# Three tiles instead of two ahead, and two gathered tiles instead of three beside the dense experts

## The reference

```python
v1, i1 = lax.top_k(s1, PEER_TOPK)
v2, i2 = lax.top_k(s2, PEER_TOPK)
cand = (v1[..., :, None] + v2[..., None, :]).reshape(nb, PEER_HEADS, PEER_TOPK * PEER_TOPK)
sc, sel = lax.top_k(cand, PEER_TOPK)
idx = jnp.take_along_axis(cidx, sel, axis=-1)
g = jax.nn.softmax(sc, axis=-1)
h = jnp.einsum('nd,nhkd->nhk', xb, u[idx]).astype(jnp.float32)
a = (jax.nn.gelu(h) * g).astype(xb.dtype)
return jnp.einsum('nhk,nhkd->nd', a, v[idx])
```

## Time and profile before

| | us |
|---|---|
| median of 3 runs | 4242.48 (4242.30 to 4243.69) |
| the profiled execution | 4242.34 |
| its span, first to last instruction | 4240.4 |
| early phases | 1 to 556 |
| late phases (projection, differential, window, merge, memory) | 556 to 1999 |
| late retrieval | 2000 to 2583 |
| experts | 2610 to 4209 |
| TensorE, VectorE, ScalarE, POOL busy | 3276.6, 3193.4, 1079.0, 1665.2 |

### The profile page before, as it was taken

The page is one execution under the profiler, slowest core; times in us unless marked ns, Lnnn a source line. Parts: engine busy times, 40 slices in busy tenths (PEclk is TensorE's granted clock), DMA queues, the critical chain, the costliest instruction groups (busy, mean ns, idle before and its releaser), DMA issues. The chain is left out here.

```text
span 4240.4 us, 46588 instructions
## 1 busy us (share of the span) xinstructions
PE 3276.6 (77%) x14797; PEld 2487.0 (59%) x14797; DVE 3193.4 (75%) x5977; ACT 1079.0 (25%) x1952; POOL 1665.2 (39%) x1349
## 2 busy tenths in 40 slices
PE   7677459986869788577645534999999999999995
PEld 6444448864547544365645534777777777777774
DVE  4311568665756487683689995999999999999997
ACT  3211121112313211111115443222222222222222
POOL 0000015653433255462000002666666666666663
PEclk9678779996975699797768878999999999999997
DMA  5222149987756787883001116999999999999996
GB/s 198 70 102 104 50 149 330 351 298 216 239 166 211 254 315 283 325 280 132 3 13 84 84 79 234 367 360 364 361 366 360 364 362 362 364 363 362 363 362 226
DMA packets 410032, 1047.07 MB, mean 247 GB/s; under 512 B 45472, under 2 KB 160800, under 8 KB 408864
## 3 DMA queue, kind: packets, MB, share of 16 engines
q0 software_dynamic: 184384, 672.09, 43.6%
q1 hardware_dynamic: 206080, 364.00, 23.9%
q10 hardware_dynamic: 19440, 9.44, 0.8%
HBM read 973.58 MB, written 72.88 MB: 247 GB/s over the span
## 5 line engine op out<-in xcount | busy, mean ns | idle before, releaser
L2059 POOL DMA_INDIRECT exp_gu<-in_peer_u_rows,exp_gidx x384 | 553.6, 1442 | 1055.8 <-DMA exp_ggate<-s_ggate 609.9
L2067 POOL DMA_INDIRECT exp_gv<-in_peer_v,exp_gidx x384 | 453.6, 1181 | 122.9 <-issue 116.8
L65 POOL DMA_INDIRECT H<-in_peer_u_rows,gidx x256 | 340.9, 1332 | 409.5 <-DVE dots L74 291.8
L2133 DVE SCALAR_TENSOR_TENSOR H<-exp_gv,exp_coef,H 128x1024 f32<-128x1024 f32 x384 | 470.7, 1281 | 14.3 <-issue 8.4
L2199 PE MATMUL exp_h<-exp_xh,exp_uh 128*128 128x512 f32 x1024 | 410.4, 401 | 89.2 <-ACT exp_gel L2088 48.9
L2123 DVE CUSTOM_DVE_ANT_0 exp_gu<-exp_gu,exp_xg 128x1024 f32<-128x1024 f32 x384 | 459.2, 1221 | 0.0
L2201 PE MATMUL exp_h<-exp_xh,exp_ul 128*128 128x512 f32 x1024 | 401.0, 392 | 0.0
L2200 PE MATMUL exp_h<-exp_xl,exp_uh 128*128 128x512 f32 x1024 | 400.0, 391 | 0.0
L74 DVE CUSTOM_DVE_ANT_0 H<-H,xg 128x1024 f32<-128x1024 f32 x256 | 301.8, 1221 | 33.1 <-DMA H<-in_peer_u_rows,gidx 32.9
L2207 PE MATMUL exp_y<-exp_vh,exp_ah 128*128 128x512 f32 x768 | 300.3, 391 | 0.0
L2208 PE MATMUL exp_y<-exp_vl,exp_ah 128*128 128x512 f32 x768 | 300.0, 391 | 0.0
(11 more groups left out here) (318 smaller groups left out, 6986.9 us busy)
## 6 DMA issues: line engine op xcount, KB each, us to landing
exp_u<-in_peer_u SPq DMA_DIRECT2D x128, 512.0 KB, 6.5
exp_v<-in_peer_v SPq DMA_DIRECT2D x128, 512.0 KB, 7.3
proj_w<-in_w_in SPq DMA_DIRECT2D x32, 1024.0 KB, 8.8
exp_w<-s_w SPq DMA_DIRECT2D x128, 256.0 KB, 6.4
out_z<-proj_zs SPq DMA_DIRECT2D x72, 256.0 KB, 5.8
merge_gates<-out_z SPq DMA_DIRECT2D x9, 1024.0 KB, 5.4
merge_wo<-in_w_out SPq DMA_DIRECT2D x2, 4096.0 KB, 29.3
top_wq<-in_w_peer_q SPq DMA_DIRECT2D x2, 4096.0 KB, 13.3
```

Source lines behind the costliest of these rows:

```text
L65: pool.indirect_dma_start(out=ring[j % len(ring)], out_offset=None, in_=table, in_offset=bass.IndirectOffsetOnAxis(ap=K["gidx"][:, u % NE, ...
L2059: pool.indirect_dma_start(out=gu[i % 2][t][:, :], out_offset=None, in_=I["peer_u_rows"], in_offset=bass.IndirectOffsetOnAxis(ap=gidx[:, t, ...
L2067: pool.indirect_dma_start(out=gv[i % 2][t][:, :], out_offset=None, in_=I["peer_v"].rearrange("a b d -> (a b) d"), in_offset=bass.IndirectO ...
L2133: dve.scalar_tensor_tensor(out=H[:, FIRST_G + t, :], in0=gv[x][t][:, :], scalar=coef[:, t:t + 1], in1=H[:, FIRST_G + t, :], op0=ALU.mult, ...
```

## The change

NE goes from 2 to 3 and NG from 3 to 2, so three tiles pass ahead, six follow, and of these two are gathered and four stay dense. The six lists of numbers are made for it: 384 dots are spread as 189, 111 and 84, and 384 axpys as 39, 189 and 156. The memory phase keeps five buffers (2 and NE). In the step of the experts the second addition now follows the last dot.

```diff
@@ -24,7 +24,7 @@
 CW = 512
 ROPED, PLAIN = 3, 5
 CHUNKS = ROPED + PLAIN + 1
-NE = 2
+NE = 3
 NKEY = 128
 
 
@@ -90,10 +90,10 @@
     return ap[:, bass.ds(c % 2, 1), 4 * half:4 * half + 4, 0:width].rearrange("p a k n -> p (a k) n")
 
 
-HIGH_AT = {2: (0, 0), 7: (3, 5)}
-LOW_AT = {2: (0, 0), 7: (4, 6)}
-LOAD_AT = {2: (1, 1), 7: (5, 7)}
-PER_TILE = (0.0, 2.0, 2.0, 2.6, 2.6, 2.6, 2.6, 2.6, 2.3)
+HIGH_AT = {3: (0, 1), 6: (2, 4)}
+LOW_AT = {3: (0, 1), 6: (3, 5)}
+LOAD_AT = {3: (1, 2), 6: (4, 6)}
+PER_TILE = (0.0, 3.0, 3.0, 4.3, 4.3, 4.3, 4.3, 4.3, 4.0)
 
 
 def phase_project(nc, sem, K, I, S, base, n, units=()):
@@ -1539,7 +1539,7 @@
                 output(n - 1)
 
 
-NG = 3
+NG = 2
 ND = NT - NE - NG
 PH = 8
 TOP = 16
@@ -2158,10 +2158,9 @@
                         add_half(q - 1, 1)
                     if further:
                         low_u(q + 2, s)
-                    dot(s, turn, 0)
-                    dot(s, turn, 1)
+                    for t in range(NG):
+                        dot(s, turn, t)
                     add_half(q, 0)
-                    dot(s, turn, 2)
                     if not first:
                         axpy(q - 1, 1 - s, turn_before)
 
@@ -2294,9 +2293,9 @@
                                base=0, pattern=[[-1, P]], channel_multiplier=1)
 
 
-DOTS = (140, 84, 32)
-AXPYS = (24, 124, 108)
-MERGE_SLOTS, MEMORY_SLOTS = 7, 3
+DOTS = (189, 111, 84)
+AXPYS = (39, 189, 156)
+MERGE_SLOTS, MEMORY_SLOTS = 7, 2
 
 
 def spans(counts):
```

## The result

The changed kernel takes 4376.82 us (median of 4 runs, 4376.38 to 4381.16), the kernel before 4243.08 on the same chip: a ratio of 1.0313, 95% interval 1.0299 to 1.0327. The profiled span went from 4240.4 to 4374.4 us, +134.0.

A forecast was written before the change was run, and what follows sets the result against it. It took VectorE to bound the experts' step, TensorE close behind, and gathers' 360 to 365 GB/s to limit the changed late phases. Early +180, late retrieval -45, late +134, experts -150: +119 on 4242.34, 4360 us; range 4260 to 4440.

The forecast's parts named there:

- the late term: Five late phases, projection to memory: losing a tile and gaining gathers, counted as bytes at the ceiling, costs +134 us.
- Experts, -150: Experts: step falls from 12.30 to 11.1 us, TensorE next at 11.0; -150 us, bounds -166 and -90.
- Early phases, +180: Early phases: a third tile with nothing beside it adds +180 us (155 to 205).
- Late projection, +28: Late projection: 129 MB at a gather ceiling of 360 GB/s set the time, 419 against 391 us.
- The first rival: Late phases: gathers land as fast as VectorE asks, late only +40, total 4267 us; chance 0.10.
- Late diff, +4: Late differential attention: 27 dots at 1.18 us mostly show, the leaving tile gives back 28; +4 us (-28 to +12).
- Late window, +35: Late window attention: 72 MB at the ceiling, 200 us, plus a start of 20; 220 against 185 us.
- merge, +40: Late merge: 117 MB at 365 GB/s, 320 against 280 us; VectorE's own bound is 314.
- Late memory, +27: Late memory: 82 MB at 365 GB/s take 225 us, then 84 us of the sample tile's chain; 309 against 282.
- Rival 2: Late phases hide the extra gathers in idle DMA and VectorE time: late -161, total 4066 us; chance 0.07.
- Rival 3: Experts keep their pace, spare bank handovers holding TensorE at 12.0 us: gain only 38, total 4473 us; chance 0.06.
- Rival 4: TensorE's clock falls where it waits for DMA: 100 us more in the projection, total 4460 us; chance 0.04.

The follow-up runs named there:

- like runs: The changed kernel with six gather buffers in the memory phase (4355.84 us) or 40 matmuls a step in the experts (4253.81 us); projection, diff and window are unchanged.
- half the columns: Changed kernel, late dots and axpys over 512 of 1024 columns, gathers whole: 4231.96 us.
- half the bytes: Changed kernel, each late gather moving 512 of its 1024 columns, VectorE's instructions as long as before: 4308.93 us.

## Why the prediction was right, and where its sizes were off

The sign, the two sides of the account and the time (4360 against 4376.82) were right. But the late term, the one with the argument in it, was 65 us short, and the experts and the early phases made up for most of it: +65 late, -33 experts, -16 early, -2 retrieval leave +15 of the span. That the time came within 17 us is in good part luck. One sum of the prediction is off: the forecast's own range, combined from its terms as stated, ends at 4436 and not at 4425.

- *Experts, -150, measured -183*, beyond the bound of -166. The mechanism held: VectorE down to 9.94 us, TensorE next at 48 matmuls, the idle time ahead of the spare bank on VectorE's side now. The mis-sized term is TensorE's pace: 0.229 us from a stretch of the earlier trace rows whose first ten starts lay 0.231 apart and the rest 0.226, 0.227 in the running step, and the 0.1 us for two semaphore waits does not exist.
- *Early phases, +180, measured +164.* Every term within 4 us but one: diff and window, 35 predicted, 22.7 measured. The third tile sees few past keys: 10.6 us in the diff.
- *Late projection, +28, measured +16.* Near the right size by the wrong step. "At the ceiling" failed: halving the bytes left the phase at 415.3 us. VectorE's dots and GpSimd's issues behind them set the pace, and the DMA engines stood one step behind; only with both relieved did it fall to 366.0. The rate of 360 to 365 GB/s was an average over queue 0's busy time, over the experts and over a stretch of 40 us, and no ceiling; 382 to 399 were reached at a share of 1.00 to 1.03. The first rival, which let the ceiling give way, was right on the rate and wrong on what would follow: the projection did not fall to TensorE's time, because another limit stood there.
- *Late diff, +4, measured +30.* The mis-sized term is the tile that left: it was priced at 28 us and was worth 10.1 without gathers, about the 10.6 that a tile cost in the early phases (the two terms of one tile should have been compared). The 27 dots cost 40 us instead of 32 in this run, but 30 and 33 in the two like runs, so their price is not refuted. The like runs differ as TensorE's clock does: 327.3, 320.2 and 316.6 us at granted clocks of 0.75, 0.77 and 0.79 over the whole phase.
- *Late window, +35, measured +48; merge, +40, measured +35.* The merge came out at the prediction's second bound, VectorE's 314 us, and not at its first: VectorE waited 3.0 us for rows, and 117 MB passed at 373 GB/s, above the 365. Each half alone gave only 8 or 13 us because the other bounds stand close. The window's 67 added gathers cost 66 us, less the tile's 18; half the columns gave 22 back, half the bytes about as much as two like runs differ by, and 17 on top of half the columns. The step that failed is the rate: 310 GB/s at a share of 0.92, where 360 was assumed.
- *Late memory, +27, measured +69*, the largest miss. The failed step is "82 MB at 365": up to the last tile's scaling the phase took 260 us instead of 225, and the steady stretch moved 299 GB/s, with five buffers. VectorE waited 66 us for rows. A sixth buffer gave 20.5 us, half the bytes 48, half the columns 23.
- *Rival 2*, that the late phases hide the gathers, is out: 1.31 us for each added one. *Rival 3* is out by the step. *Rival 4* came true on a small scale: the projection's granted clock went from 0.95 to 0.88. Behind the 8.25 us gap the matmuls started 0.43 us apart for 4 us, near the lower of the clock's two levels (1.2 GHz), before the pace of 0.233 us was back: some nine matmuls by 0.2 us, 2 us for this gap. Over the phase the 1422 matmuls kept TensorE busy 318 us, and 303 without gathers: 15 us and not 100. In the diff it is more: 224 us for 876 matmuls at 0.75, and 173 without gathers at 0.93. There VectorE's busy time grew by 124 of the 133 us that the gathers cost, so what the clock adds to the path was not separated.

The Trainium skill's 425 GB/s ("DMA: Bandwidth & Descriptors", section "Bandwidth") was not reached here either; the most that a stretch of 200 us or more shows is 399.

What stays open: how much of the 143 us that shorter VectorE instructions give back is the instructions themselves and how much the faster issue of gathers behind them. A kernel that lifts only the issue was not tried. Nor was one that puts the projection's weight split ahead of the dots in VectorE's line, which would test whether its 46.0 us of TensorE's idle time are a matter of order alone.

## What to carry to other kernels

Work that is moved under other work is priced by a run without it, phase by phase, in the kernel at hand: here the first 512 gathers cost 0.37 us each and the next 256 cost 1.31, when most of the cover was filled and a tile of it gone. Before a rate is called a ceiling, look at the highest rate at a full share, and at who issues the transfers: a share of 1.00 was true here and still not the bound. When a term and its mirror image both stand in a sum (a tile taken out here and put in there), compare them.

## What the hardware showed

The issue of an indirect gather on GpSimd waits for the VectorE instruction that is running when it begins, if that one reads two tensors from SBUF. Over the 768 late gathers of the changed kernel: the 91 that began while VectorE was idle took 0.93 to 0.94 us. Of 215 that began during a dot, over 0.03 us behind its start, 214 took what was left of the dot plus 0.81 us, to within 0.03, and never under 0.93: behind a dot with 0.56, 0.87 or 1.17 us left the issue took 1.37, 1.68 and 1.98. The same sum fits 248 of 252 that began during an axpy. During the weight split of 2.29 us the longest of 16 took 3.06. Of the 16 that began during the maxima of the diff (TENSOR_REDUCE, whose one input lies in PSUM) none took over 0.94, nor did one that began in the first hundredths of a microsecond of a dot. Two tensors are not the only case: two issues that began during a scaling of H (L1387, one tensor from SBUF) took 1.20 and 1.36, by the same sum. The Trainium skill has the rule: in "SBUF — State Buffer", section "Who interferes with whom", a VectorE instruction with two SBUF inputs contends with a GpSimd instruction that reads SBUF, through a port pair that is an exclusive lock. The trace agrees: the remainder of VectorE's instruction is added in full, and the issue of a gather behaves as an instruction that reads SBUF. Where the same section infers that a tensor_tensor does not stall a DMA issued from GpSimd, the trace differs, and the measurement decides: the weight split is a tensor_tensor.
